# Transposing h itself and applying the pre-norm weights by partition in a 1-core hybrid decoder trunk

## What is computed

```python
f = swiglu(rmsnorm(h, ffn1_pre_g[i]), ffn1_w_in[i], ffn1_w_down[i])
h = h + 0.5 * rmsnorm(f, ffn1_post_g[i])
hn = rmsnorm(h, mix_pre_g[i])
mixed = (gmlp + ssd, concatenated) @ hyb_w_out     # layer 0
mixed = mla_attention(hn, ...)                      # layer 1
h = h + rmsnorm(mixed, mix_post_g[i])
f = swiglu(rmsnorm(h, ffn2_pre_g[i]), ffn2_w_in[i], ffn2_w_down[i])
h = h + 0.5 * rmsnorm(f, ffn2_post_g[i])
gate = jax.nn.sigmoid(rmsnorm(h, ple_pre_g[i]) @ ple_w_gate[i])
h = h + rmsnorm(gate * (p[i] @ ple_w_proj[i]), ple_post_g[i])
```

## Time and profile before

| | us |
|---|---|
| median of 3 runs | 1134.64 |
| lowest, highest | 1133.79, 1135.49 |
| the profiled execution's own time | 1133.96 |
| its span | 1132.2 |
| PE busy | 1107.9 (98%) |
| DVE busy | 817.4 (72%) |
| ACT busy | 565.5 (50%) |
| POOL busy | 86.4 (8%) |

### The profile page before, as it was taken

How to read it: one execution, slowest core, us unless ns; L and a number is a source line. 1 busy time by engine, 2 the same in 40 slices (tenths; PEclk the granted TensorE clock), 3 DMA queues, 4 the chain that set the end, 5 groups by cost and what they waited for, 6 DMA issues and landing times.

```text
span 1132.2 us, 14058 instructions
## 1 busy us (share of the span) xinstructions
PE 1107.9 (98%) x5713; PEld 935.3 (83%) x5713; DVE 817.4 (72%) x1053; ACT 565.5 (50%) x692; POOL 86.4 (8%) x124
## 2 busy tenths in 40 slices
PE   8999999999999999999999999999999999999997
PEld 5888888788788788888887888888888878888885
DVE  5867777588997677777775867767865667776774
ACT  7444444567464554444555544446655555444443
POOL 2000000201210200000022000001200020000012
PEclk9999999999999999999999999999999999999999
DMA  9555555645543565555565555554523365555541
GB/s 319 207 196 193 186 186 177 240 178 186 186 167 128 192 219 192 197 196 188 183 205 191 209 186 186 190 189 170 195 75 113 112 222 196 186 189 191 195 169 56
DMA packets 31168, 207.83 MB, mean 184 GB/s; under 512 B 3713, under 2 KB 3761, under 8 KB 7681
## 3 DMA queue, kind: packets, MB, share of 16 engines
q1 hardware_dynamic: 27648, 194.00, 48.2%
q0 software_dynamic: 3456, 12.94, 3.4%
HBM read 205.86 MB, written 1.06 MB: 183 GB/s over the span
## 4 chain that ended last, share of the span: by engine, by line
PE 62%; DVE 10%; ACT 3%; issue 2%; POOL 1%; DMA 0%; DVEq 0%; POOLq 0%; ACTq 0%
PE PS L604 17%; PE PS L189 10%; PE PS L191 10%; PE PS L190 10%; PE PS L607 9%; DVE WL L171 4%; ACT WH L164 1%; PE PS L371 1%; PE PS L1727 1%; PE PS L1726 1%; DVE hn L1336 1%; PE PS L1745 1%; PE PS L1735 0%; PE PS L1027 0%; DVE ca L1291 0%
## 5 line engine op out<-in xcount | busy, mean ns | idle before, releaser
L171 DVE TENSOR_TENSOR WL<-raw,WH 128x2048 fp32r<-128x2048 f32 x181 | 413.3, 2289 | 155.2 <-ACT WH L164 155.1
L164 ACT ACTIVATE WH<-raw 128x2048 fp32r<-128x2048 f32 x181 | 344.9, 1908 | 119.2 <-DMA raw<-stream 119.2
L604 PE MATMUL PS<-X,WH 128*128 128x512 f32 x1152 | 288.3, 392 | 0.0
L604 PEld LDWEIGHTS PS<-X,WH 128*128 128x128 f32 x1152 | 209.1, 189 | 38.8
L607 PEld LDWEIGHTS PS<-X,WL 128*128 128x128 f32 x1152 | 157.1, 190 | 11.3
L607 PE MATMUL PS<-X,WL 128*128 128x256 f32 x1152 | 160.6, 282 | 0.0
L189 PE MATMUL PS<-WH,X 128*128 128x512 f32 (+1 forms) x352 | 139.9, 397 | 7.7 <-DVE WL L171 5.8
L706 ACT ACTIVATE sgb<-sgb 128x256 f32<-128x256 f32 x72 | 30.1, 418 | 227.9 <-DVE sgb L702 227.9
L191 PE MATMUL PS<-WL,X 128*128 128x512 f32 (+1 forms) x352 | 136.9, 389 | 0.0
L190 PE MATMUL PS<-WH,X 128*128 128x512 f32 (+1 forms) x352 | 136.8, 389 | 0.0
L189 PE MATMUL PS<-WH,BH 128*128 128x512 f32 x288 | 113.1, 393 | 0.0
(11 more groups left out here) (274 smaller groups left out, 1313.3 us busy)
## 6 DMA issues: line engine op xcount, KB each, us to landing
raw<-stream SPq DMA_DIRECT2D x181, 1024.0 KB, 4.8
PG<-post_g POOLq DMA_DIRECT2D x8, 512.0 KB, 6.6
QG<-pre_g POOLq DMA_DIRECT2D x7, 512.0 KB, 7.3
raw<-stream SPq DMA_DIRECT2D x4, 512.0 KB, 8.1
Eg<-acs_rows POOLq DMA_DIRECT2D x2, 1024.0 KB, 6.1
h<-x SPq DMA_DIRECT2D x2, 512.0 KB, 5.8
out<-h SPq DMA_DIRECT2D x4, 256.0 KB, 2.1
wsT<-gm_w POOLq DMA_DIRECT2D x1, 512.0 KB, 9.2
```

The costliest lines, as they stand in the source:

```text
L164: act.activation(WH[:, n % RING, :], raw[:, n % RING, :], ACT.Copy).then_inc(sem("w_hi"), 1)
L171: dve.tensor_tensor(WL[:, n % RING, :], raw[:, n % RING, :], WH[:, n % RING, :], ALU.subtract).then_inc(sem("w_lo"), 1)
L604: pe.matmul(PS[:, bank, :], wh[:, kt, cols], X[:, kt, :, :].rearrange("p a n -> p (a n)"), start=kt == 0, stop=False)
```

## The change

Six things are done together.

1. h itself is transposed in all stages. `normed`, QG and its seven broadcasts are gone. The pre-norm weights of all stages lie in one tile qg_cols (128 x 64, one column for each 128 rows of x), and x_high and x_low apply them by partition in four instructions of 128x128 a half.
2. At a boundary DVE's order changes: the split of unit m+2 moves into `behind` of t = 1, between mean and update; the split of m+3 stands between the halves of x_low of t = 1. Behind a ple stage, the tail of the kernel too, its products are made alternately with `gained`.
3. The row 1/rms of the feed-forward stages is made without PE: POOL writes the two columns to DRAM (512 bytes each), waits for them, and loads them back broadcast over the partitions.
4. In stage 0 x is loaded in four halves, the transposes are spread over the first products, and the squares stand on both sides of the split of unit 2.
5. Hybrid stage: dt in 8 matmuls of 512 columns (high and low weights side by side in 32 columns, high and low x side by side), summed by four small f32 matmuls with a doubled identity `both`; the copy of xs goes, the multiplication with D is made by DVE from PSUM inside `times_dt`; times_dt(1) stands before the split of u+16; weigh(0, 0) moves behind gate_v(1), and segment(1, 1) before weigh(1, 0).
6. Attention: the transposes of the latents one step earlier; waits for the emptied banks later; ACT takes Q2 and Q3 before exponentials(2j+3) instead of behind; DVE splits unit u+7 behind maxima and normalise of head 3 instead of before.
In the three pairs of lists below a row is the instruction's number in its engine's order, its line, operation, written and read tiles, and the semaphores it waits for.

The diff, cut to its core:

```diff
-        QG = place("QG", [P, D])
+        qg_cols = place("qg_cols", [P, NS * KT])
...
+        rs_mem = nc.dram_tensor("rs_mem", (SEQ,), f32, kind="Internal").ap()
...
-            if stages[s][0] == "ple":
-                ple_product(dve, s, t, 0)
-                ple_product(dve, s, t, 1)
             for b in range(2):
+                if stages[s][0] == "ple":
+                    ple_product(dve, s, t, b)
                 gained(dve, s, t, b)
             post_mean(dve, s, t)
             if between is not None:
@@ -341,17 +343,8 @@
             dve.wait_ge(sem("post_rs"), 2 * s + t + 1)
             for b in range(2):
                 update_h(dve, s, t, b)
-                if s + 1 < NS:
-                    normed(dve, s + 1, t, b)
-
-
-
-        def normed(dve, s, t, b):
-            h_ready(dve, s, t, b)
-            if (t, b) == (0, 0):
-                dve.wait_ge(sem("qg"), 16 * s)
-            dve.tensor_tensor(hn[:, t, half(b)], h[:, t, half(b)], QG[:, half(b)], ALU.mult)\
-               .then_inc(sem("hn_done"), 1)
...
-                    pe.wait_ge(sem("hn_done"), 4 * (s - 1) + 2 * t + a_ + 1)
+                    h_ready(pe, s, t, a_)
                 else:
-                    pe.wait_ge(sem(f"x_loaded{t}"), 16)
+                    pe.wait_ge(sem(f"x_in{t}{a_}"), 16)
                 for q in range(4):
                     kt = 4 * a_ + q
                     ins = pe.transpose(PS[:, x_bank(s, t, a_), q * P:(q + 1) * P],
-                                       (hn if s else h)[:, t, kt * P:(kt + 1) * P], ident[:, :])
+                                       h[:, t, kt * P:(kt + 1) * P], ident[:, :])
...
         def x_high(act, s, t, halves=(0, 1)):
             for a_ in halves:
-                act.wait_ge(sem("x_tr"), 4 * s + 2 * t + a_ + 1)
-                act.activation(x_half(XH, t, a_), x_psum(s, t, a_), ACT.Copy).then_inc(sem("x_hi"), 1)
+                if (s, t, a_) == (0, 0, 0):
+                    act.wait_ge(sem("qg_cols"), 16)
+                act.wait_ge(sem("x_tr"), halves_done(s, t, a_))
+                for kt in range(4 * a_, 4 * a_ + 4):
+                    ins = act.activation(x_tile(XH, t, kt), x_psum(s, t, kt), ACT.Copy, scale=pre_gain(s, kt))
+                ins.then_inc(sem("x_hi"), 1)
...
         def x_low(dve, s, t, halves=(0, 1)):
             for a_ in halves:
-                dve.wait_ge(sem("x_hi"), 4 * s + 2 * t + a_ + 1)
-                dve.tensor_tensor(x_half(XL, t, a_), x_psum(s, t, a_), x_half(XH, t, a_), ALU.subtract)\
-                   .then_inc(sem("x_lo"), 1)
...
+                dve.wait_ge(sem("x_hi"), halves_done(s, t, a_))
+                for kt in range(4 * a_, 4 * a_ + 4):
+                    ins = dve.scalar_tensor_tensor(x_tile(XL, t, kt), x_psum(s, t, kt), pre_gain(s, kt),
+                                                   x_tile(XH, t, kt), ALU.mult, ALU.subtract)
+                ins.then_inc(sem("x_lo"), 1)
...
-            post_square(act, s - 1, 1)
-            if stages[s - 1][0] == "ple":
-                split_to(m + 3)
+            post_square(act, s - 1, 1, (lambda: split_to(m + 3)) if stages[s - 1][0] == "ple" else None)
...
         def boundary_dve(dve, s, done, split_to):
             m = first[s] if s < NS else n_units
-            from_ple = stages[s - 1][0] == "ple"
-            split_to(m if from_ple else m + 1)
+            before = stages[s - 1][0]
+            split_to(m if before == "ple" else m + 1)
             behind(dve, s - 1, 0)
             if s == NS:
                 behind(dve, s - 1, 1)
                 return
             x_low(dve, s, 0, (0,))
-            if from_ple:
+            if before == "ple":
                 split_to(m + 1)
             x_low(dve, s, 0, (1,))
-            if stages[s][0] != "mla":
-                split_to(m + 2)
-            behind(dve, s - 1, 1, (lambda: split_to(m + 3)) if from_ple else None)
             if stages[s][0] == "mla":
+                behind(dve, s - 1, 1)
                 x_low(dve, s, 1, (0,))
                 return
-            x_low(dve, s, 1)
+            if before == "ple":
+                split_to(m + 2)
+            behind(dve, s - 1, 1, lambda: split_to(m + 3 if before == "ple" else m + 2))
+            x_low(dve, s, 1, (0,))
             split_to(m + 3)
+            x_low(dve, s, 1, (1,))
...
-        def rs_row_pe(pe, s):
-
-            pe.wait_ge(sem("pre_rs"), 2 * s + 2)
-            for t in range(2):
-                ins = pe.matmul(PS[:, 6, tok(t)], col(s, t, RS).broadcast_to([P, P]), ident[:, :], start=True, stop=True)
-            ins.then_inc(sem("rs_tr"), 1)
...
+        def rs_row_pool(pool, s, f):
+
+            pool.wait_ge(sem("pre_rs"), 2 * s + 2)
+            for t in range(2):
+                pool.dma_start(rs_mem[tok(t)].rearrange("(p n) -> p n", n=1), col(s, t, RS)).then_inc(sem("rs_out"), 16)
+            pool.wait_ge(sem("rs_out"), 32 * (f + 1))
+            pool.dma_start(rs_row[:, :], rs_mem.partition_broadcast(P)).then_inc(sem("rs_there"), 16)
...
-                ins = product(pe, PS[0:HEADS, P1, 0:SEQ], dt_hi[:, kt, :], dt_lo[:, kt, :], XH[:, kt, :], XL[:, kt, :],
-                              kt == 0, kt == KT - 1)
+                ins = pe.matmul(PS[0:2 * HEADS, P1, :], dt_parts[:, kt, :, :].rearrange("p a h -> p (a h)"),
+                                X[:, kt, :, :].rearrange("p a n -> p (a n)"), start=kt == 0, stop=kt == KT - 1)
             ins.then_inc(sem("hy_dtp"), 1)
             gemm(4, (0,))
             pe.wait_ge(sem("hy_dtc"), 1)
+            pe.wait_ge(sem("hy_both"), 1)
             for t in range(2):
-                ins = pe.transpose(PS[:, P1, t * HEADS:(t + 1) * HEADS], dtT[:, tok(t)], ident[0:HEADS, 0:HEADS])
+                for part in range(2):
+                    ins = pe.matmul(PS[:, P1, t * HEADS:(t + 1) * HEADS], dtT[:, part * SEQ + t * P:part * SEQ + (t + 1) * P],
+                                    both[:, :], start=part == 0, stop=part == 1)
...
             def times_dt(t):
-                dve.wait_ge(sem("hy_xs"), t + 1)
+                dve.wait_ge(sem("hy_back"), t + 1)
+                dve.tensor_tensor(heads(xs[:, t, :]), heads(flat_pair(CT)), per_head(DV, HEADS, 64), ALU.mult)\
+                   .then_inc(sem("hy_skip"), 1)
...
             times_dt(0)
             split_to(u + 15)
             normalise(0)
+            times_dt(1)
             split_to(u + 16)
-            times_dt(1)
             normalise(1)
...
-            skip(0)
             pool.wait_ge(sem("hy_rows"), 16)
             rows(0)
-            skip(1)
...
-                if j == 1:
-                    wait_emptied(Q2)
-                if j == 2:
-                    wait_emptied(Q3)
...
+                if j == 1:
+                    wait_emptied(Q2)
...
+                if j == 2:
+                    wait_emptied(Q3)
...
+                if j < 2:
+                    take((Q2, Q3)[j])
                 if j < 7:
                     exponentials(2 * j + 3)
-                if j < 2:
-                    take((Q2, Q3)[j])
...
-                split_to(u + 7 + j)
+                if j:
+                    split_to(u + 7 + j)
                 if j < 7:
                     maxima(2 * j + 3)
                     normalise(2 * j + 3)
+                split_to(u + 7 + j)
...
-            sp.dma_start(h[:, 0, :], a["x"][tok(0), :]).then_inc(sem("x_loaded0"), 16)
-            sp.dma_start(qg_cols[:, :], a["pre_g0"]).then_inc(sem("qg_cols"), 16)
+            def load_x(t, b):
+                sp.dma_start(h[:, t, half(b)], a["x"][tok(t), half(b)]).then_inc(sem(f"x_in{t}{b}"), 16)
+
+            load_x(0, 0)
+            sp.dma_start(qg_cols[:, :], a["pre_g"]).then_inc(sem("qg_cols"), 16)
             load_part(0, 0)
             load_part(0, 1)
-            sp.dma_start(h[:, 1, :], a["x"][tok(1), :]).then_inc(sem("x_loaded1"), 16)
+            load_x(1, 0)
+            load_x(0, 1)
+            load_x(1, 1)
```

## The result

The changed kernel takes 1155.85 us (median of 5 runs, 1153.94 to 1158.47) against 1134.06 for the kernel before on the same chip: a ratio of 1.0189, 95% interval 1.0173 to 1.0204. The forecast was 1134.0, with a range up to 1137.0, and it was wrong by size and by case: what happened is the rival called "the late row", to which it gave one chance in ten and 6 us.

A forecast was written before the change was run, and what follows sets the result against it. TensorE, busy 98% of the span, was taken as the bound. Opening -0.6, row -1.8, hybrid -1.4, tail -0.3, boundaries +1.7 and attention +1.8 sum to -0.6: 1134.64 becomes 1134.0 us, range 1130.2 to 1137.0.

The forecast's parts named there:

- the late row: Feed-forward block 0: 1/rms lands over 13 us after its root; 3 us late gives +6, 1140; chance 0.10.
- The row: Feed-forward stages: 1/rms through DRAM takes 13 to 14 us against 14.2, costed at nothing, bound +2 a stage.
- TensorE's saving on the row: Four feed-forward stages: 1/rms no longer made on TensorE, 0.45 us each, -1.8 in all.
- The boundaries: Seven stage starts: longer chain to x delays first products, partly repaid by waits that go; +1.7 us together.
- the tail's -0.3: End of kernel: the mean waits for the square instead of a second gained multiply, -0.3 us.
- The opening: Stage 0: third unit's WL begun before pre_square's second half, so its product starts at 23.95, not 24.55; -0.6 us.
- The hybrid stage: Hybrid mixer: fewer TensorE products and a removed wait, -1.4 us in sum, between -0.7 and -2.3.
- dt: Hybrid mixer: eight products of 512 columns replace 24 of 256, small matmuls give back 0.3; -0.7 us.
- The wait of 1.52: Hybrid mixer at 298.00: times_dt(1) ahead of WL(u+16) removes it; 0.7 us of the gain kept.
- The attention loop: Head pairs 0 and 1: new order delays CL and the output products, +1.8 us, ends -0.5 and +2.2.
- A: Whole kernel: only removals count, new stalls replacing waits TensorE had anyway; 1131.0 us, chance 0.30.
- B: Same as the late row: feed-forward block 0, each microsecond past 2 of slack paid four times; 1140, chance 0.10.

The follow-up runs named there:

- this part alone: Changed kernel without the 1/rms row, hybrid and attention parts, leaving h transposed, pre-norm weights by partition, boundary order and opening: 1135.34 us, ratio 1.0009.
- the hybrid kernel: The kernel before with only the hybrid stage's part of the change: 1133.11 us, ratio 0.999.

## Why the prediction was wrong

**The row.** This is the step that failed: "it is just hidden ... I cost it at nothing, with its bound at +2 a stage". The sum of DMA times was worked from the nearest rows, but the nearest by queue and not by shape: 32 pieces of 512 bytes for 256 of 4. The write took 10.5 for 4.0. I had written the path's length as 13 to 14 us against 14.2 at hand, and still gave it a tenth; and the price of 6 us had neither the held-up weight stream nor the clock in it. Measured, the four steps are +20.9. Of these 8.2, in stage 4, did not come through the row at all but through a weight unit that landed late; for what the writes do to their neighbours the prediction had no term. TensorE's saving on the row came out at 0.36 a stage in the starts side by side, not the 0.45 forecast.

**The boundaries** were right in their pieces. The chain of x costs what the two rows of the opening said:

```profile
200.75 0.50 PE L189 MATMUL PS<-WH,X 128*128 128x512 f32 x1 [0.56 <-DVE X L404]
...
210.68 0.50 PE L189 MATMUL PS<-WH,X 128*128 128x512 f32 x1 [0.56 <-DVE X L404]
```

The shift grows by 0.72 and 0.81 at these two and falls by 1.03 at 211.39, where 0.7, 0.8 and 1.0 were forecast; into stages 2 and 6 they are 0.8, 0.8 and 1.0. The sum of +1.7 stands at +1.8 in the trace with this part alone, and the tail's -0.3 at -0.3.

**The opening** is not the -0.6 forecast, nor anything steady. Behind the product that waited at 24.55 the shift was -0.2 in the changed kernel and +0.7, -1.0, +0.1 and -1.0 in four kernels with the same opening; in two kernels with the old opening it was -0.8 and +0.4. A term of 0.6 is smaller than that scatter.

**The hybrid stage** was forecast at -1.4 and measures -1.1 in the runs and -1.2 in its part of the trace, but by luck: two errors cancel. dt was to give -0.7 and gave -0.1, since the eight products save 0.9 and the small f32 matmuls behind them take 0.75 of it back, not 0.3. The wait of 1.52 did go, and some 1.1 of it was kept, not 0.7.

**The attention loop** was right as a mechanism and mis-sized: "+1.8 in all" against 3.1. The first stall came out at +1.1 (848.01 less the shift of 14.7 is 833.3; the forecast said 833.14). The rest is the half clock behind it, 1.6, which the term did not have and which two of the kernels with this stall did not pay.

**The rivals.** A needed absent stalls, and they were there. B was the case. Its sign of recognition, gsum's scaling ending a wait of TensorE in block 1, is the first row of the waits, in three of the four stages. Its price did not follow from its own rule: 3 us late with 2 of slack, paid four times, is +4 and not +6.

## What to carry to other kernels

Before a value goes through DRAM, ask in what pieces it is written: a column over 128 partitions is 128 writes of 4 bytes, and no row of a transfer with longer pieces prices it; nor does its price end at its own latency when a weight stream uses the same engines. A hand-over that saves 0.36 us of TensorE a stage is not worth a path whose length is as long as the time at hand. And a new long stall of TensorE is to be priced with a possible half clock behind it: in the changed kernel the stalls of 2.4 to 5.8 us behind the opening cost some 1.6 to 2.5 us more than their length, those of 0.6 to 0.8 at the boundaries their length alone.

Before the shift between two traces is put down to an edit, take off what stands there ahead of it: the -2.0 at the end of the hybrid kernel's trace holds 0.8 from an opening that the edit left alone.

## What the hardware showed

- Writes of 4-byte pieces into DRAM: 8.8 us to landing for 0.5 KB, against 4.6 for the same pieces into SBUF and 4.0 for 16 KB in 512-byte pieces; the 1 MB weight units beside them took 10.2 to 12.6 us to land in stage 2, against 4.7 to 4.8 with the row on TensorE and nothing else under way. The DMA engines were as busy as before and moved 44 GB/s for 6 us. A second write issued 4 to 6 us behind the first, which was still under way, took 14.7 to 16.1.
- The granted clock fell to its lower level (0.50 of 2.4 GHz) behind idle times of 3.3, 5.8, 2.6 and 2.4 us in the changed kernel, and stayed at full level where products into an unused bank filled them. It did not fall behind the 2.8 us in the opening. The length of the idle time does not settle it: behind the same 2.6 us in the attention loop the clock fell in four kernels and not in two (0.50 from 848 to 850 in the changed kernel, 1.00 from 845 to 847 in the one with TensorE kept busy), and behind 1.84 us in stage 0 it fell with the writes in stage 0 alone (0.50 from 46 to 48), not in the changed kernel behind 1.85 (1.00).
- POOL's root of 128x1, 0.55 us in 16 of 16 cases before, took 2.52 to 2.53 at six of the boundaries, where VectorE's split of a weight unit (two SBUF inputs, 2.28 us) now runs beside it:

```profile
203.13 2.28 DVE L171 TENSOR_TENSOR WL<-raw,WH 128x2048 fp32r<-128x2048 f32 x1
```

```profile
203.29 2.53 POOL L325 TENSOR_TENSOR stat<-stat,nhalf 128x1 f32<-128x1 f32 x1 [7.11 <-DVE stat L318]
```

It began 0.16 behind the split and ended 0.41 behind its end. The Trainium skill, "SBUF — State Buffer", section "SBUF: two separate sides", calls the port pair that the two engines share an exclusive lock for a whole instruction; this row agrees. The wait was off TensorE's path here, since the update behind it was ready in time, but a short POOL operation on a chain should not be put beside such a split.
